# An expert gate table summed in cleared memory by one-word accumulating transfers, and the low parts of the up tiles moved to VectorE

## What is computed

```python
def peer_ffn(h, w_query, sub_keys, expert_u, expert_v):   # 8 heads, 128 x 128 experts, top 16
    s1, s2 = ...                          # scores of two sets of 128 keys, for each token and head
    v1, i1 = lax.top_k(s1, 16)
    v2, i2 = lax.top_k(s2, 16)
    cand = v1[..., :, None] + v2[..., None, :]            # 16 x 16 candidates
    cidx = i1[..., :, None] * 128 + i2[..., None, :]
    sc, pos = lax.top_k(cand, 16)
    eidx = take_along_axis(cidx, pos)                     # 16 experts for each token and head
    g = jax.nn.softmax(sc, axis=-1)                       # their gates
    a = einsum(expert_u[eidx], h)
    act = gelu(a) * g
    return einsum(act, expert_v[eidx])
```

## Time and profile before

| what | value |
| --- | --- |
| median of 3 runs | 3030.32 us (3025.0 to 3035.52) |
| span of the profiled execution, first to last instruction | 3005.5 us |
| median of the runs less that span | 24.8 us |
| PE busy | 2977.4 us, 99% |
| DVE, ACT, POOL busy | 56%, 42%, 48% |
| granted PE clock | 0.998 of full speed |
| DMA moved | 473.18 MB, 157 GB/s |

### The profile page before, as it was taken

How to read it: one execution, slowest core, us unless ns; L and a number is a source line. 1 busy time by engine, 2 the same in 40 slices (tenths; PEclk the granted TensorE clock), 3 DMA queues, 4 the chain that set the end, 5 groups by cost and what they waited for, 6 DMA issues and landing times.

```text
span 3005.5 us, 40609 instructions
## 1 busy us (share of the span) xinstructions
PE 2977.4 (99%) x15170; PEld 2562.3 (85%) x15170; DVE 1692.1 (56%) x2918; ACT 1269.3 (42%) x2109; POOL 1450.7 (48%) x747
## 2 busy tenths in 40 slices
PE   9999999999999999999999999999999999999998
PEld 7887888888888888899999997778888889888887
DVE  5826359998999701068888875363121436631223
ACT  6555344335777633333333334353233334532332
POOL 6731443444444444577878503644444443444442
PEclk9999999999999999999999999999999999999999
DMA  4242332444677765599999953213333322123332
GB/s 147 93 139 79 105 101 85 136 141 135 181 209 201 211 195 168 189 327 371 361 377 360 375 192 117 80 64 98 94 96 98 110 70 71 49 92 98 98 98 85
DMA packets 331163, 473.18 MB, mean 157 GB/s; under 512 B 125764, under 2 KB 235236, under 8 KB 330488
## 3 DMA queue, kind: packets, MB, share of 16 engines
q1 hardware_dynamic: 308472, 403.79, 41.8%
q0 software_dynamic: 22528, 67.19, 6.0%
HBM read 405.97 MB, written 60.86 MB: 155 GB/s over the span
## 4 chain that ended last, share of the span: by engine, by line
PE 95%; issue 1%; DVE 1%; POOL 1%; DMA 1%; ACT 0%; SPq 0%; DVEq 0%; POOLq 0%; ACTq 0%
PE pb L893 29%; PE pb L894 29%; PE pb L895 29%; PE pb L1223 2%; PE pb L1516 1%; PE pb L1074 1%; POOL s_over L753 0%; PE pb L1173 0%; PE pb L1102 0%; PE pb L1357 0%; PE pb L1377 0%; PE pb L1041 0%; PE pb L941 0%; PE pb L1278 0%; DMA s_ring<-ev 0%
## 5 line engine op out<-in xcount | busy, mean ns | idle before, releaser
L753 POOL TENSOR_TENSOR s_over<-s_ring,s_rhigh 128x1024 fp32r<-128x1024 f32 x401 | 999.6, 2495 | 1362.4 <-ACT s_rhigh L1624 1361.7
L1624 ACT ACTIVATE s_rhigh<-s_ring 128x1024 fp32r<-128x1024 f32 x525 | 555.3, 1059 | 1086.4 <-DMA s_ring<-w 498.6
L893 PE MATMUL pb<-s_over,s_rhigh 128*128 128x512 f32 (+1 forms) x2392 | 876.7, 367 | 0.9 <-DVE s_over L2471 0.8
L895 PE MATMUL pb<-s_over,s_over 128*128 128x512 f32 (+1 forms) x2392 | 872.8, 365 | 0.0
L894 PE MATMUL pb<-s_over,s_rhigh 128*128 128x512 f32 (+1 forms) x2392 | 872.7, 365 | 0.0
L893 PE MATMUL pb<-s_hS,s_rhigh 128*128 128x512 f32 (+1 forms) x1664 | 649.8, 390 | 3.6 <-DVE s_hS L2782 2.5
L895 PE MATMUL pb<-s_hS,s_over 128*128 128x512 f32 (+1 forms) x1672 | 645.0, 386 | 0.0
L894 PE MATMUL pb<-s_hS,s_rhigh 128*128 128x512 f32 (+1 forms) x1664 | 641.7, 386 | 0.0
L893 PEld LDWEIGHTS pb<-s_over,s_rhigh 128*128 128x128 f32 x2392 | 449.1, 188 | 56.0 <-issue 1.3
L895 PEld LDWEIGHTS pb<-s_over,s_over 128*128 128x128 f32 x2392 | 449.0, 188 | 53.2
L894 PEld LDWEIGHTS pb<-s_over,s_rhigh 128*128 128x128 f32 x2392 | 449.1, 188 | 52.9 <-issue 1.0
(11 more groups left out here) (310 smaller groups left out, 3166.9 us busy)
## 6 DMA issues: line engine op xcount, KB each, us to landing
s_ring<-w SPq DMA_DIRECT2D x272, 512.0 KB, 3.5
s_ring<-eu SPq DMA_DIRECT2D x128, 512.0 KB, 4.0
s_ring<-ev SPq DMA_DIRECT2D x128, 512.0 KB, 6.2
acts<-s_arena SPq DMA_DIRECT2D x128, 256.0 KB, 4.0
s_arena<-acts SPq DMA_DIRECT2D x128, 192.0 KB, 5.2
s_arena<-gates SPq DMA_DIRECT2D x128, 192.0 KB, 6.6
gates<-s_arena SPq DMA_DIRECT2D x36, 512.0 KB, 5.0
gates<-s_arena SPq DMA_DIRECT2D x6, 1024.0 KB, 7.5
```

What stands on the lines that cost most here:

```text
L753: gp.tensor_tensor(rlow[:, s, :, :], ring[:, s, :, :], rhigh[:, s, :, :].bitcast(F32), ALU.subtract).then_inc(S("w_split"), 1)
L893: mm(dst, a_high, b_high, start=start, stop=False)
L895: return mm(dst, a_low, b_high, start=False, stop=stop)
L1624: sc.activation(rhigh[:, s, :, :], ring[:, s, :, :], ACT.Copy).then_inc(S("w_high"), 1)
```

## The change

The table is no longer made on PE.

- **Clearing.** POOL fills a small tile `zero` (128 x 256) at the start. SP writes it to the whole table in 24 DMAs of 1 MB (rows of 1 KB), one behind each of the tiles T_GATE + 4 to T_GATE + 27.
- **Per head.** The exponential and the normalization are done head by head (`gate_exp` on ACT, one before the up tiles and seven between GELUs, each with a table load before it and one behind it; `gate_scale` on DVE), and DVE also works out each gate's address in the table (`g_at`).
- **Adding.** POOL issues 8 x 3 x 16 = 384 indirect DMAs (head, block of 128 tokens, pick). Each adds one word from each of 128 partitions at its own address in `gates`. A block's 16 DMAs of head h wait until its DMAs of the heads before have landed (`g_put`).
- **Removed.** The 12 transposes and 384 table matmuls on PE, the one-hots, drains and the 42 table DMAs.
- **Low parts.** POOL splits up tiles 0 and 1 only; DVE takes tiles 2 to 127 and the first four expert tiles, the first 52 of them one by one between the steps of the top-k (`low_beside`: four in head 1, eight in heads 2 to 7).
- **Reading back.** `act_in` of rows 0 to 3 stands behind the wait for all 384 DMAs, after the last up tile's load; those of rows 4 to 7 stand behind the loads of the first four expert tiles.

```diff
@@ sync @@
+            sp.wait_ge(S("zeroed"), 1)
+            for q in range(ZQ):
+                tile(T_GATE + RING + q, a["w"][T_GATE + RING + q])
+                sp.dma_start(gzero[q], zero[:, :].unsqueeze(1).to_broadcast([P, NK * NK * TD // (ZQ * P * ZW), ZW]))\
+                    .then_inc(S("table_zero"), 16)
...
-                if part < 7 and 0 <= b < TD // GB:
-                    i0, i1 = G_PART[part:part + 2]
-                    sp.wait_ge(S("gb_copied"), (b + 1) * (GB // 4))
-                    sp.dma_start(gtab[i0:i1, :, b * GB:(b + 1) * GB].rearrange("n p t -> p n t"), gbuf[:, b % 2, i0:i1, :])\
-                        .then_inc(S(f"gates_out{b % 2}"), 16)
...
+            for t in range(TT - 1):
+                sp.wait_ge(S(f"g_put{t}"), 16 * PH * TOPK)
+            for e in range(4):
+                sp.wait_ge(S(f"a_out{e}"), 32)
+                act_in(e, e)
@@ gpsimd @@
-            splits(T_QUERY, T_U + 120)
+            splits(T_QUERY, U_LOW)
+            gp.wait_ge(S("table_zero"), 16 * ZQ)
+            for h in range(PH):
+                gp.wait_ge(S("gate_done"), h + 1)
+                for t in range(TT - 1):
+                    if h >= 1:
+                        gp.wait_ge(S(f"g_put{t}"), 16 * TOPK * h)
+                    for k in range(TOPK):
+                        n = h * TOPK + k
+                        gp.indirect_dma_start(gate1, bass.IndirectOffsetOnAxis(ap=g_at[:, t, n:n + 1], axis=0),
+                                              score[:, t, h, k:k + 1], None, compute_op=ALU.add)\
+                            .then_inc(S(f"g_put{t}"), 16)
@@ tensor @@
-            for t in range(TD):
...
-                pe.wait_ge(S("oh_low"), t + 1)
-                mm(pb[:, 4 + (t // 2) % 4, (t % 2) * 2 * P:(t % 2 + 1) * 2 * P], oh2[t // 8 % 2][:, t % 8, :],
-                   oh1[:, t % 16, :, :].rearrange("p e i -> p (e i)"), start=True, stop=True).then_inc(S("oh_used"), 1)
-                if t % 8 == 7:
-                    up(T_U + U_TOP + t // 8, U_TOP + t // 8)
-            for k in range(U_REST, NK):
+            for k in range(NK):
                 up(T_U + k, k)
@@ scalar @@
+            for k in range(NK):
                 gelu(k)
+                h, r = divmod(k - LOWS_1 + LOWS, LOWS)
+                if r == 0 and h < PH:
+                    gate_exp(h)
+                if k >= 125:
+                    for e in ((0, 1), (2, 3), (4, 5, 6, 7))[k - 125]:
+                        gated_high(e)
@@ vector @@
+            def low_beside(i, at):
+                if i == 0:
+                    return
+                if i == 1 and at < 8 - LOWS_1:
+                    return
+                if lowered[0] == U_LOW:
+                    ve.wait_ge(S("w_split"), U_LOW)
+                low_next()
...
+            while lowered[0] < T_V:
+                low_next()
             for k in range(8):
                 gated(k)
                 if k >= 1:
                     gated_low(k - 1)
+                if k % 2:
+                    low_next()
```

More of the change, by code:

```diff
@@ L98 @@
 T_END = T_F1 + 64
-U_TOP = 36
-U_GATE = TD // 8
-U_REST = U_TOP + U_GATE
+U_LOW = T_U + 2
+LOWS_1, LOWS = 4, 8
 W_QKNA, W_QKD = 0, 8
@@ L435, in program @@
         pabf = C.take(2, 64)
[L436 removed]
+        choice = C.take(2, TT, 16)
         score = C.take(TT, PH, TOPK)
[L438 to L446 removed]
+        gsum = C.take(TT)
+        chosen = C.take(TT, P)
+        g_at = C.take(TT - 1, P, dt=U32)
+        g_atf = C.take(TT - 1, 16)
+        gneg = C.take(2, TT, 16)
+        tok = C.take(TT)
         s_row = C.take(P, dt=U32)
@@ L689, in _ @@
                 act_out(124 + r)
+                sp.wait_ge(S("e_raw"), r + 1)
+                act_in(4 + r, 4 + r)
             for e in range(4):
@@ L818, in pick_act @@
                     .then_inc(S(f"s_act{j // 16 % 2}"), 16)
-            gp.wait_ge(S("gate_sum"), 13)
-            for e in range(2):
-                gp.wait_ge(S(f"gates_out{e}"), 7 * 8 * (TD // GB))
+            gp.wait_ge(S("s_listed"), 4)
             for j in range(6):
                 fetch_row(j)
-            splits(T_U + 120, T_V + RING)
             for e in range(4):
@@ L1761, in _, with gate_exp @@
             mean_root(1)
+            def gate_exp(h):
+                sc.wait_ge(S("gate_neg"), h + 1)
+                sc.activation(gneg[:, h % 2, :, :], gneg[:, h % 2, :, :], ACT.Exp).then_inc(S("gate_exp"), 1)
             for i in range(PH + 1):
@@ L1783, in _ @@
                     m.then_inc(S("s_copied"), 1)
+                if i == 6:
+                    gate_exp(0)
             def gelu(k):
@@ L2354, in _ @@
                     .then_inc(S("tk_step"), 1)
+                low_beside(i, 3)
+                if i >= 1:
+                    gate_scale(i - 1)
                 ve.wait_ge(S("tk_step"), 4 * i + 2)
```

225 lines of the change are left out of this document (71 added, 154 removed).

## The result

The changed kernel takes 3048.56 us (median of four runs, 3043.2 to 3053.74), the kernel before beside it 3031.92. The ratio is 1.0058, 95% interval 1.0041 to 1.0075: **slower, by 16.6 us**. The prediction was 2983 us and faster; the time lies above its whole range. What came true is rival A: GpSimd became the bound.

A forecast was written before the change was run, and what follows sets the result against it. PE, busy 99% of the span with 95% of the last chain, was taken as the bound. PE's -50.4, clearing +1, VectorE 0, GpSimd 0 and expert-stage start +2 made -47.4: 3030.3 to 2983 us, range 2974 to 3039 us.

The forecast's parts named there:

- rival A: Adds on GpSimd become the bound, slower than before: 3103 us at 2.1 us an issue, 3553 at 3.27; chance 0.19.
- What PE gives up: Up stage: transposes and table matmuls leave PE, all on the path, saving 50.4 us; last GELU near 1223 us.
- Clearing the table: Up stage: 24 DMAs of 1.05 MB behind tile loads, needing 315 GB/s; +1 us, bounds 0 and 17.
- VectorE: Top-k heads 2 to 7: added splits and small operations take 41.5 us of 43.5 a head; expected cost 0.
- Rival B: Slow clearing or late DVE eats part of the gain before the up stage ends: 2992 to 3021 us; chance 0.14.
- The upper end of that paragraph: DVE in heads 2 to 7: at 48.1 us a head it falls 4.6 us a head behind, costing +17 us.
- Start of the expert stage: Gate reads and row 7 delay the load of expert tile 4: +2 us, bounds 0 and 6.
- GpSimd: 384 adds in the up stage start at 519 us and end at 1139, 63 us early: no cost.
- the limit: GpSimd's adds must average at most 1.76 us an issue to finish before SP's wait at 1201.8 us.
- I take the median: Adds take the one-word gather's median, 1305 ns, plus 0.30 us between issues: 1.6 us an issue.
- The bounds of that paragraph: GpSimd's adds: cheapest 1.25 us an issue, ending at 1005 us; dearest 3.27 us, ending at 1781.
- 24.8 us lie outside; I take them as unchanged: Whole kernel: profiled span 3005.5 us against the runs' median 3030.32; the difference was taken as lying outside the span.

The follow-up runs named there:

- kernel of 384 paced writes: The changed kernel with all 384 transfers written, not added, and a small GpSimd clearing behind each and behind the first 40 one-word gathers: 2955.48 us, ratio 0.9833.
- both are paced: A small GpSimd clearing behind the first 40 one-word gathers, nothing else: changed kernel 3027.49 us, ratio 0.9989; kernel before 3005.06 us, ratio 0.9916.
- the repeat: The kernel before, run and profiled again with no edit: span 3023.9 us, its execution 3025.73 us.
- the unpaced writes: The changed kernel with the addition taken off all 384 transfers, so each overwrites its word, and no clearings between: 3270.56 us, ratio 1.0796.

## Why the prediction was wrong, step by step

**What PE gives up: right.** 50.4 us were predicted, all of it on the path. In the kernel of 384 paced writes, where GpSimd is in time, the GELUs run for 1223.3 - 532.4 = 690.9 us, as forecast, against 741.3 before:

```profile
L1788 ACT ACTIVATE s_arena<-pb x128: 580/598/604, 532.4 to 1223.3; 128x512 f32<-128x512 f32 x128
```

Its median is 2955.5 us against 3005.9, where neither has a stop: 50.4 us again. That comparison holds every other term too, so the others add up to about nothing, where the sum had +3.

**Clearing the table: right.** PE is busy throughout 300 to 375 us and has no wait there; the DMA engines are at 0.99 and 316 GB/s, the rate that I had asked of them, so the +1 was nearer 0. (Before, the same 75 us had a share of 0.32.)

**VectorE: right.** PE never waits for its split among up tiles 6 to 53. Rival B has nothing for it. (The upper end of that paragraph had a slip, without effect: six heads at 4.6 us are 27.6 us, not 25.)

**Start of the expert stage: within its bounds of 0 to 6 us, rather under the +2.** In the paced writes PE has one wait there, of 1.2 us, where before had 0.8.

**GpSimd: the step that failed.** The start was right (519.8 us against 519), the point at which SP would ask too (1202.9 against 1201.8), and so was the limit, 1.76 us an issue. What failed is the sentence "I take the median": 1.6 us, from the one-word gathers of the earlier trace rows plus the 0.30 of the earlier trace rows. The adds (min/median/max ns, first and last start us):

```profile
L805 POOL DMA_INDIRECT gates<-s_arena x384: 1546/1547/2609, 519.8 to 1267.7; - x192
```

The very least is 1.55 + 0.30 = 1.85 us, over the limit of 1.76 with no contention at all; the mean is (1269.2 - 519.8)/384 = 1.95. I had taken the gather's median as holding the price of a crowded stage, and it did; but the quiet price of an add is 0.6 us above the gather's 0.94. The run with the addition removed shows where that lies: a write has a median of 958 ns. The bounds of that paragraph, 1.25 and 3.27, did hold the value; the limit of 1.76 lay low between them. With one bound 0.5 us under the limit and the other 1.5 above it, a chance of 0.19 for the upper side had no row behind it. The median of another kind of transfer is no row for this one.

Contention comes on top. 632.6 us of issues less 384 x 1.547 are 38.5 us, 0.10 an issue. They decided the sign: without them after would have taken some 3010 us beside before's 3032 (an estimate, 3048.6 - 38.5). The quiet price alone would have eaten more than half of the gain; the contention made it a loss. Of the 384 adds 57 lasted over 1.6 us, and 56 of these began while VectorE ran an operation with two inputs in SBUF (42 splits, 14 steps of the top-k); none of the 243 that began while VectorE ran nothing did:

```profile
989.76 2.40 POOL L805 DMA_INDIRECT gates<-s_arena  x1 [0.30 <-issue]
...
1005.63 1.55 POOL L805 DMA_INDIRECT gates<-s_arena  x1 [0.30 <-issue]
```

```profile
989.52 1.23 DVE L2290 TENSOR_TENSOR s_over<-s_ring,s_rhigh 128x1024 fp32r<-128x1024 f32 x1 [3.92 <-ACT s_rhigh L1603]
...
1005.65 1.23 DVE L2290 TENSOR_TENSOR s_over<-s_ring,s_rhigh 128x1024 fp32r<-128x1024 f32 x1 [3.60 <-ACT s_rhigh L1603]
```

The first add starts 0.24 us into a split and lasts 0.85 longer than the least; the second starts 0.02 us before one and loses nothing. The Trainium skill, "SBUF — State Buffer", section "SBUF: two separate sides", has the pair of ports locked by whichever starts first, also by a VectorE operation with two inputs in SBUF against a GpSimd one that reads SBUF; the trace agrees with one half. An add that begins inside a split loses the more the earlier it begins (1.0 us at 0.08 to 0.10 into it, 0.19 at 0.91). But the splits don't wait for adds: 94 of them began inside an add and took 1.21 to 1.25 us, as long as those that didn't. The prediction had cited the section for copies and scalar operations only, and had missed that the splits which the change moves to VectorE are the kind that it names.

**Rival A: came true, and its formula came near.** It had the gain gone at 1.91 us an issue; 1.95 was measured. By its working the end at 1271 is 60 us past the 1211 at which PE starts to wait, so 2983 + 60 = 3043 us; measured 3048.6. The rest is the restart, for which it allowed 12 us (1223 less 1211): it was 20 us from SP's release to the first matmul, so that PE waited 66.8 us and not 60, and then came matmuls at half clock (0.32 us each from 1291 to 1294 and from 1298 to 1301, where 0.17 is the pace). The Trainium skill's 2.0 us for each transfer ("DMA: Bandwidth & Descriptors", section "Anatomy of one DMA — SWDGE (gpsimd) path") gave some 3065. I had set it aside because transfers overlap, and they do (a write every 1.26 us is issued); the near agreement is chance, since the 1.95 us are issue time on GpSimd and not a transfer's fixed cost.

**"24.8 us lie outside; I take them as unchanged": wrong, with no effect on the sign.** 1.8 lie outside. The rest was the second stop, which the profiled execution of before didn't have. It happens to be of like size in after (3046.0 - 3025.0 = 21.0 us, against 25.7 in before), so the medians differ by nearly what they differ by without it: -50.4 of PE, +67 for the first stop with its restart (16.6 + 50.4). Where both are paced, 3027.5 against 3005.1, it is -50.4 + 72.8.

## What to carry to other kernels

Size a new kind of transfer by a run or by both of its bounds, never by the median of a neighbouring kind; where the limit lies between the bounds, the forecast is a coin, however good the other terms. Where an engine stops for no wait that the profile names while GpSimd issues indirect transfers densely, try spreading them out: with a clearing of 0.33 us behind each, one every 1.46 us, no stop was seen here, and at one every 1.25 us the other engines all but stopped in most executions on three chips of four. Behind adds, which come every 1.85 us anyway, a clearing of one column only cost time. Try the same on the kernel before, or its gain is put down to the change. Put nothing behind a wait in SP's queue that doesn't need it: moving four loads ahead of the wait halved the restart (20.6 to 10.5 us on one chip).

## What the runs showed of the hardware

- **Issue time of an indirect transfer of one word for each of 128 partitions**, plus 0.30 us to the next: gather 0.94 us, write 0.96, add 1.55. The add also moves more packets: 77824 in the software queue with 384 adds, 34816 with 384 writes, 144 and 32 for each transfer over the 22528 of the gathers.
- **Starving by rate.** At a period of 1.25 to 1.26 us the other engines slow down after 20 to 40 transfers and are back at full pace 8 to 17 us after GpSimd pauses. At 1.36 it happened in one profiled execution, at 1.46 and at 1.85 in none. The rate isn't all of it: the first profile of before, without a stop, has its gathers as dense as the repeat with one (29 starts between 1280 and 1319.5 us in both). The DMA engines are nearly idle in the worst stretches (0.02), so it isn't bandwidth. In 50 us of such a stop, 900 to 950 us of the unpaced writes, these are the only queues with packets (packets, MB, share):

```profile
q1 hardware_dynamic: 288, 0.79, 4.8%
q0 software_dynamic: 1280, 0.02, 1.9%
```

  The instruction queues have none there; the same 50 us of the paced writes show them:

```profile
q8 instruction: 2, 0.03, 0.2%
```

  The Trainium skill, "Runtime: NRT & Kernel Launch", section "Instruction fetch mechanics", says that each engine's sequencer fetches its instructions over a DMA queue of its own. That fits, but it is weak: PE ran only a matmul every 2.1 to 2.8 us in these 50 us and so needed few new instructions, and from 700 to 750 us, which hold most of another such stop, both instruction queues moved a packet. No run shows what holds the engines, so the mechanism stays open. That pacing takes the stop away is shown on one chip (3030.8 to 3005.1 us in before, and in the profiles of after); the 3270.6 against 2955.5 us of the writes are from two chips.
- Before's stop came in nearly all executions on three chips and in none of 20 on a fourth, by their times. A single profile of a kernel can lack 20 us that its median has: compare its own time with the median before building on it.
